# A two-layer encoder trunk in float32 halves: products of the down projection moved behind the up columns, VectorE reordered in two steps, a later fetch of parameters

## The reference

```python
def swiglu(x, w_gate, w_up, w_down):
    return (jax.nn.silu(x @ w_gate) * (x @ w_up)) @ w_down

for l in range(DEPTH):                                   # DEPTH = 2
    x = layer_norm(ALPHA * x + 0.5 * swiglu(x, ffn1_w_gate[l], ffn1_w_up[l], ffn1_w_down[l]), ln1_g[l], ln1_b[l])
    h = x @ w_in[l]
    ...                                                  # stick-breaking heads and chunked heads
    x = layer_norm(ALPHA * x + mixed @ w_out[l], ln2_g[l], ln2_b[l])
    x = layer_norm(ALPHA * x + 0.5 * swiglu(x, ffn2_w_gate[l], ffn2_w_up[l], ffn2_w_down[l]), ln3_g[l], ln3_b[l])
```

## Time and profile before

| | |
|---|---|
| median of 3 runs (lowest, highest) | 1031.84 us (1031.26, 1035.53) |
| the profiled execution | 1034.74 us |
| its span in the trace | 1033.1 us |
| granted TensorE clock, mean | 0.993 of full speed |
| busy: PE, PEld | 1002.7 us (97%), 925.7 us (90%) |
| busy: DVE, ACT, POOL | 814.4 us (79%), 568.6 us (55%), 31.1 us (3%) |

### The profile page before, as it was taken

How to read it: one execution, slowest core, us unless ns; L and a number is a source line. 1 busy time by engine, 2 the same in 40 slices (tenths; PEclk the granted TensorE clock), 3 DMA queues, 4 the chain that set the end, 5 groups by cost and what they waited for, 6 DMA issues and landing times.

```text
span 1033.1 us, 18653 instructions
## 1 busy us (share of the span) xinstructions
PE 1002.7 (97%) x7020; PEld 925.7 (90%) x7020; DVE 814.4 (79%) x882; ACT 568.6 (55%) x616; POOL 31.1 (3%) x54
## 2 busy tenths in 40 slices
PE   6799999999999999999989999999999999999998
PEld 6799999799987899999878999997999888999996
DVE  4988886854778898986869888868457879898968
ACT  5455554457775555554456555545576855555545
POOL 2100000001100000000010000000011000000000
PEclk9899999999999999999989999999999999999999
DMA  8646454454315555454445556544633265555451
GB/s 331 249 166 223 182 190 164 163 205 153 128 66 185 186 223 203 165 214 188 166 166 204 208 178 220 188 141 163 216 111 123 82 233 211 188 183 203 166 181 62
DMA packets 34088, 185.33 MB, mean 179 GB/s; under 512 B 3824, under 2 KB 3824, under 8 KB 18928
## 3 DMA queue, kind: packets, MB, share of 16 engines
q1 hardware_dynamic: 32400, 174.60, 46.9%
q0 software_dynamic: 1488, 9.45, 2.5%
q10 hardware_dynamic: 144, 0.52, 0.1%
HBM read 183.51 MB, written 1.05 MB: 179 GB/s over the span
## 4 chain that ended last, share of the span: by engine, by line
PE 87%; DVE 6%; DMA 3%; issue 3%; ACT 1%; SPq 0%; DVEq 0%; ACTq 0%
PE bank L1048 26%; PE bank L1049 25%; PE bank L1050 25%; PE bank L1146 6%; DMA raw<-stream 3%; PE bank L1110 2%; DVE w_lo L703 2%; PE bank L1103 1%; DVE w_lo L720 1%; DVE stick_t L711 1%; ACT w_hi L422 1%; PE bank L1291 1%; DVE w_lo L734 1%; DVE soft_t L853 0%; DVE w_lo L727 0%
## 5 line engine op out<-in xcount | busy, mean ns | idle before, releaser
L1048 PE MATMUL bank<-xT_hi,w_hi 128*128 128x256 f32 x1568 | 446.0, 284 | 9.6 <-DVE soft_t L853 6.6
L1049 PE MATMUL bank<-xT_lo,w_hi 128*128 128x256 f32 x1568 | 444.3, 283 | 0.0
L1050 PE MATMUL bank<-xT_hi,w_lo 128*128 128x256 f32 x1568 | 444.3, 283 | 0.0
L703 DVE TENSOR_TENSOR w_lo<-raw,w_hi 128x2048 fp32r<-128x2048 f32 x122 | 278.5, 2290 | 81.4 <-ACT w_hi L422 81.4
L1048 PEld LDWEIGHTS bank<-xT_hi,w_hi 128*128 128x128 f32 x1568 | 301.5, 192 | 15.0 <-issue 12.1
L422 ACT ACTIVATE w_hi<-raw 128x2048 fp32r<-128x2048 f32 x122 | 232.7, 1912 | 143.9 <-PE bank L1050 138.6
L1049 PEld LDWEIGHTS bank<-xT_lo,w_hi 128*128 128x128 f32 x1568 | 301.4, 192 | 2.9
L1050 PEld LDWEIGHTS bank<-xT_hi,w_lo 128*128 128x128 f32 x1568 | 301.3, 192 | 0.0
L1048 PE MATMUL bank<-w_hi,h_hi 128*128 128x512 f32 x284 | 112.0, 395 | 3.5 <-DVE h_lo L873 3.5
L1049 PE MATMUL bank<-w_lo,h_hi 128*128 128x512 f32 x284 | 112.1, 395 | 0.0
L1050 PE MATMUL bank<-w_hi,h_lo 128*128 128x512 f32 x284 | 111.2, 392 | 0.0
(11 more groups left out here) (137 smaller groups left out, 1176.3 us busy)
## 6 DMA issues: line engine op xcount, KB each, us to landing
raw<-stream SPq DMA_DIRECT2D x110, 1024.0 KB, 5.0
raw<-stream SPq DMA_DIRECT2D x110, 512.0 KB, 4.5
lnp<-ln_gb POOLq DMA_DIRECT2D x6, 1024.0 KB, 5.0
band<-rel_band POOLq DMA_DIRECT2D x2, 1024.0 KB, 8.6
xn<-x POOLq DMA_DIRECT2D x1, 1024.0 KB, 7.6
out<-xn SPq DMA_DIRECT2D x4, 256.0 KB, 2.0
qT<-xT SPq DMA_DIRECT2D x1, 512.0 KB, 4.9
qT<-xT ACTq DMA_DIRECT2D x1, 512.0 KB, 5.1
```

Source lines behind the costliest of these rows:

```text
L703: nc.vector.tensor_tensor(w_lo[:, at(slot)], raw[:, slot, :], w_hi[:, at(slot)].bitcast(F32), ALU.subtract).then_inc(lo_ready, 1)
L1048: nc.tensor.matmul(o, w[0], x[0], start=start, stop=False, skip_group_check=again)
L1049: nc.tensor.matmul(o, w[0], x[1], start=False, stop=False, skip_group_check=again)
L1050: return nc.tensor.matmul(o, w[1], x[0], start=False, stop=stop, skip_group_check=again)
```

## The change

Four edits:

```diff
@@ TensorE, step(j)
                     pe.wait_ge(lo_part, 2 * n + 2)
                     product(4, start, finished)
+                    up(j, bank[0])
                     product(3, start, m_done if stop else parts_used)
-                    up(j, bank[0])
                     pe.wait_ge(lo_ready, split(l, base + 3 * j + 4))
@@ TensorE, up(j, into)
-                    pe.wait_ge(silu_done, it(l, f, j) + 2)
+                    if into is bank[0]:
+                        pe.wait_ge(silu_done, it(l, f, j) + 2)
@@ VectorE, ffn: steps 0 and 1 written out, the loop starts at 2
-                with dve.Fori(0, SF - 1) as j:
+                for j in range(2):
+                    split_last_parts_lo(l, base + 3 * j + 4)
+                    if j == 0:
+                        split_lo(l, base + 3 * j + 5, 2)
+                        weight_sums(l, f, j + 1, FILLED[base + 1] + 2 + j)
+                    else:
+                        weight_sums(l, f, j + 1, FILLED[base + 1] + 2 + j)
+                        split_lo(l, base + 3 * j + 5, 2)
+                    gated(j + 1, 3 * j + 3, bank[0])
+                    h_sums(j + 1)
+                    split_pure_lo(l, f, j + 1)
+                    split_differences_lo(l, f, j + 1)
+                    low_h(j + 1)
+                    split_lo(l, base + 3 * j + 6, 0)
+
+                with dve.Fori(2, SF - 1) as j:
                     split_last_parts_lo(l, base + 3 * j + 4)
@@ GpSimd, at the start of each layer
             with pool.Fori(0, DEPTH) as l:
+                wait_alone(lo_ready, split(l, 15))
                 load_lnp(l, 0)
```

## The result

The changed kernel takes 1115.21 us (median of 4 runs, 1114.75 to 1117.84) against 1031.88 us (median of 4, 1031.26 to 1035.53): a ratio of 1.0808, with a 95% interval of 1.0781 to 1.0835. It is 8% slower; the forecast was 1111 us. The profiled execution took 1115.61 us, its span is 1113.9 us, its mean granted clock 0.963 (before 0.993). It lies 0.4 us above its median, while the profiled execution of the kernel before lies 2.9 us above its own, so spans compared between the two make the difference 2.5 us too small.

What follows compares the result with a forecast made beforehand. TensorE was taken to bound the kernel, without a gap in the middle steps. 61.9 + 29.8 - 7.5 - 1.8 - 3.0 = 79.4 us slower than the 1031.84 us median gave 1111 us, range 1072 to 1128.

Steps and rivals of the forecast that it cites:

- The hole: Steps 2 to 7 of each FFN: gate columns wait 2.49 us for `gated`, 24 times, 61.9 us slower.
- The clock: Gate columns behind the new waits: half clock 20 of 24 times, 1.49 us each, 29.8 us slower.
- The rival in which the clock mostly stays: The waits in steps 2 to 7 come, but the granted clock mostly holds: 1081 to 1090 us, chance 0.20.
- The gains: FFN starts and ends and the second layer's start: 12.3 us faster in all.
- the FFN starts: Steps 0 and 1: `gated` ahead of L720 and L727 removes four waits, 7.5 us faster, bounds 4 and 8.5.
- the last up columns: End of each FFN: the up columns no longer wait for a silu, 1.8 us faster, bounds 0 and 3.7.
- the later parameters: Parameters fetched in step 3: wait without releaser at second layer's start shortens, 3 us faster, between none and 6.7.
- The transfers: Rival: the next down unit is fetched later and weight sums wait in 24 steps, 38 us more, 1149, chance 0.04.

Runs made afterwards that it cites:

- the first experiment: Changed kernel with `gated` and the hidden sums ahead of the low halves of pure parts and differences in steps 2 to 7 too: 1022.93 us, ratio 0.9908.
- The fourth experiment: Changed kernel with only the low half of the differences put behind `gated` and the hidden sums in steps 2 to 7: 1056.37 us, ratio 1.0237.

## Why the prediction was right

**The hole.** Predicted 24, each 2.49 us and read as 2.32; found 24, 2.48 us in the step shown, read as 2.27 to 2.33. The chain went as written: L426 at U + 0.90 (predicted 0.89), `gated` at U + 4.27, gate columns at U + 5.23 (predicted 5.24). The move alone and the first experiment show it from both sides.

**The clock.** Predicted 20 half clocks of 1.49 us behind the holes; found 22. In the second and fourth FFN each costs what was said (gate columns 7.32 to 7.35 us, 7.33 in the earlier trace rows); in the first they took up to 7.47, and a step costs 20.52 - 16.32 = 4.20 us there, of which I had 4.07. That it would be 20 of 24 was a bet on one row out of four, and it came out well: holes of the same length left the clock alone twice here. One comparison in the forecast was off too: the longest of the holes that left the clock alone was shorter than the new ones by 0.63 us (2.32 - 1.69), both as the profile reads them, not by 0.8. The fourth experiment, with holes half as long and no half clock behind them in its profiled execution, shows that in a step that repeats the falls go with the longer hole. The rival in which the clock mostly stays, 1081 to 1090 us, was wrong. The Trainium skill, "TensorE: Matmul & The Clock Gate", section "Why this matters for your kernels", warns of idle gaps above about 3 us between bursts of matmuls. The trace goes further: here gaps of 2.3 us were followed by the half clock 22 times of 24.

**The gains.** Predicted 12.3 us. The costs by the trace are 24 x 2.48 for the holes and 22 x 1.6 for the clock (4.07 to 4.20 a step less 2.48), 94.7 us. The medians differ by 83.3, so the gains are 11.4. (The spans of the two profiled executions differ by 80.8, which would make them 13.9; but the one before was 2.9 us above its median.) The run with the move undone agrees: it keeps the gains and has no holes, and is 11.0 us faster than the kernel before. Term by term:
- the FFN starts were forecast at 7.5 us; the order alone, measured by itself, brings 7.7 (7.0 by the medians). Right, though the term took the 6.6 us of waits as the profile reads them, each 0.17 us short.
- the last up columns were forecast at 1.8 us. Alone they bring 2.8. In the changed kernel it is more, by the 1.2 us that the products at the end of the FFNs no longer wait: product 3 behind the up columns lets VectorE reach the last `gated` earlier. This I had not counted. It is the one place at which the move was seen to help, and it is too small to be seen in the time (1013.66 with the move against 1012.66 without).
- the later parameters were forecast at 3 us; alone they bring nothing (-0.1% to +0.1%). That step failed, and the size taken between two ends was a guess. The wait without releaser at the second layer was not the parameters' doing: it was as long with the fetch moved, and went when TensorE did not jump back to the head of its loop. Writing out the loop was not tried with the parameters in their old place.

In the gains the misses cancel, by luck: 3 us too much for the parameters, some 2 too little for the last up columns. What is left adds up: costs 3 us above the forecast's 91.7, nearly all of it the two half clocks more, and gains 0.9 below its 12.3. The forecast difference was 79.4 us; the medians differ by 83.3, and 1111 was 4 us short.

The transfers did not fall behind. VectorE's waits for a stream transfer in front of the weight sums even shrank, from 18.1 us in seven to 14.1 us in four; the first line is of the kernel before, the second of the changed one:

```profile
DVE stick_t L710 <- DMA raw<-stream: 18.1, 7, 6.0
```

```profile
DVE stick_t L711 <- DMA raw<-stream: 14.1, 4, 5.6
```

## What to carry to other kernels

When a matmul is moved past others at no cost to TensorE, follow the signal it raises: here nothing was added, and a `parts_used` that came 5.8 us later (L426 at 8.72 us after the gate columns' end, 94.58 - 85.86; before 72.87 - 69.92 = 2.95) reached TensorE again through a copy on ScalarE and the order on VectorE. An in-order engine should take first what the busiest engine waits for, and behind it what waits for that engine; if an order is changed to allow a move, it has to be changed in every step, the loop's too. Holes that recur must be priced with the clock behind them: 24 holes of 2.48 us cost 95 us here, not 60, while 24 of half the idle cost no clock in the execution that was profiled.

## What the runs showed of the hardware

The length of a single hole does not settle whether the clock falls: behind one of 2.32 us it stayed at 1.00 (gate columns at 414.69 in the changed kernel), behind one of 1.75 us it fell (granted clock 0.51, the run with the later fetch alone), and behind one of 1.90 us in that same execution, and one of 1.69 us, it stayed. Where holes of 2.3 us came in every step, it fell behind nearly all of them, 22 of 24 and 29 of 32; in the changed kernel it fell, once it had in an FFN, behind every later hole of that FFN, but in the run with the move alone it stayed behind the last hole of the second FFN after six falls. Behind 24 holes of 1.2 us it never fell in the execution profiled.

A loop that jumps back over a whole layer's code cost TensorE 3.1 to 3.8 us of wait, once in each run. Behind it the clock stood at 1.2 GHz for up to 6.8 us, but not always: in the run with half a hole the wait was 3.1 us and the clock stayed at 1.00. Written out, with the same matmuls in the same order, the kernel was 5.8 us faster for TensorE and, with ScalarE and VectorE, 3.8 us more (by the ratios).
